# Hybrid GLA, attention and RG-LRU backbone on one core: the recurrent blocks' input scale by another formula, and separate waits for their two gate buffers

## The reference, cut to what matters

```python
def lru_coeffs(x, w_gates, b_gates, lam):
    xb = x.reshape(b, n, LRU_BLOCKS, LRU_BW)                 # 8 blocks of 128 channels
    z = jnp.einsum('bnhi,ghij->gbnhj', xb, w_gates).reshape(2, b, n, w) + b_gates[:, None, None, :]
    gate_r, gate_i = jax.nn.sigmoid(z[0]), jax.nn.sigmoid(z[1])
    log_a = -LRU_C * gate_r * jax.nn.softplus(-lam)
    u = jnp.sqrt(-jnp.expm1(2.0 * log_a)) * (gate_i * x)
    return jnp.exp(log_a), u
# and then, per channel and in each of the two directions: h = a * h + u
```

## Time and profile before

| what | value |
|---|---|
| time, median of 3 runs (lowest to highest) | 2126.31 us (2124.08 to 2127.26) |
| the profiled execution: its own time / its span | 2122.79 us / 2121.0 us |
| mean granted TensorE clock | 0.973 |
| PE busy | 1978.5 us, 93% of the span |
| DVE busy | 1132.7 us, 53% |
| ACT busy | 939.3 us, 44% |
| POOL busy | 48.9 us, 2% |

### The profile page before, as it was taken

One profiled execution on the slowest core, in us unless ns is written; L12 is line 12 of the kernel. 1 busy time (PEld: TensorE's weight loads), 2 busy tenths in 40 slices (PEclk: granted clock), 3 DMA queues, 4 the chain that ended last, 5 costly groups with the idle time before them and its releaser, 6 DMA issues.

```text
span 2121.0 us, 26328 instructions
## 1 busy us (share of the span) xinstructions
PE 1978.5 (93%) x10944; PEld 1608.7 (76%) x10944; DVE 1132.7 (53%) x1615; ACT 939.3 (44%) x1301; POOL 48.9 (2%) x65
## 2 busy tenths in 40 slices
PE   4999999999999999699999998899899988989997
PEld 1878766777787777477777785778677887979997
DVE  2566455544645432555555324675555667657864
ACT  2343344454644322333333323443344777446653
POOL 1000000000000000000000000000000101000000
PEclk8999999999999999899999999999999999999999
DMA  7211111132333544245444522222212444544563
GB/s 283 60 60 50 55 50 40 50 98 91 99 95 102 175 172 160 78 143 175 169 159 162 177 90 79 60 70 60 66 60 74 150 144 135 170 129 155 184 185 104
DMA packets 67511, 244.98 MB, mean 116 GB/s; under 512 B 7600, under 2 KB 8640, under 8 KB 67264
## 3 DMA queue, kind: packets, MB, share of 16 engines
q1 hardware_dynamic: 64544, 233.86, 33.8%
q0 software_dynamic: 1696, 5.24, 0.8%
q10 hardware_dynamic: 1152, 4.19, 0.5%
HBM read 242.21 MB, written 1.05 MB: 115 GB/s over the span
## 4 chain that ended last, share of the span: by engine, by line
PE 81%; DVE 10%; ACT 5%; issue 2%; DMA 1%; SPq 0%; ACTq 0%; DVEq 0%
PE ps L1258 62%; PE ps L1248 4%; PE ps L1534 2%; PE ps L1189 2%; PE ps L1444 2%; DVE wlo L742 1%; PE ps L1278 1%; DMA wraw<-in_weights 1%; ACT whi L399 1%; DVE state L1002 1%; PE ps L1465 1%; PE ps L1198 1%; PE ps L1358 1%; PE ps L1368 1%; PE ps L1345 1%
## 5 line engine op out<-in xcount | busy, mean ns | idle before, releaser
L742 DVE TENSOR_TENSOR wlo<-wraw,whi 128x1024 fp32r<-128x1024 f32 x352 | 433.4, 1233 | 517.0 <-ACT whi L399 516.5
L399 ACT ACTIVATE whi<-wraw 128x1024 fp32r<-128x1024 f32 x352 | 370.5, 1055 | 387.4 <-PE ps L1258 241.1
L1258 PE MATMUL ps<-hh,whi 128*128 128x512 f32 (+1 forms) x1760 | 415.9, 359 | 33.2 <-DVE hl L859 23.9
L1258 PE MATMUL ps<-hl,whi 128*128 128x512 f32 (+1 forms) x1760 | 398.9, 349 | 0.0
L1258 PEld LDWEIGHTS ps<-hh,whi 128*128 128x128 f32 x1760 | 292.7, 193 | 109.5 <-issue 65.5
L1258 PE MATMUL ps<-hh,wlo 128*128 128x512 f32 (+1 forms) x1760 | 366.5, 349 | 1.6 <-DVE wlo L742 1.6
L1258 PEld LDWEIGHTS ps<-hl,whi 128*128 128x128 f32 x1760 | 296.2, 193 | 42.1 <-issue 1.9
L1258 PEld LDWEIGHTS ps<-hh,wlo 128*128 128x128 f32 x1760 | 287.2, 192 | 44.1 <-issue 4.4
L770 DVE SCALAR_TENSOR_TENSOR fa<-ps,par,fa 128x510 f32<-128x510 f32 (+1 forms) x176 | 100.0, 610 | 14.9 <-ACT fa L462 13.4
L1258 PE MATMUL ps<-bh,whi 128*128 128x512 f32 (+1 forms) x384 | 85.8, 346 | 4.4 <-ACT whi L399 4.4
L462 ACT ACTIVATE fa<-ps,par 128x512 f32<-128x512 f32 (+1 forms) x88 | 53.9, 663 | 69.6 <-PE ps L1258 69.5
(11 more groups left out here) (206 smaller groups left out, 2424.7 us busy)
## 6 DMA issues: line engine op xcount, KB each, us to landing
wraw<-in_weights SPq DMA_DIRECT2D x352, 512.0 KB, 3.6
wada<-in_w_ada SPq DMA_DIRECT2D x80, 512.0 KB, 4.1
ada_first<-in_w_ada ACTq DMA_DIRECT2D x8, 512.0 KB, 18.7
ada_first<-in_w_ada SPq DMA_DIRECT2D x8, 512.0 KB, 20.1
wgate<-in_w_gate POOLq DMA_DIRECT2D x16, 256.0 KB, 2.8
x<-in_xt SPq DMA_DIRECT2D x1, 2048.0 KB, 10.1
out_x<-x SPq DMA_DIRECT2D x1, 1024.0 KB, 4.5
par<-in_params POOLq DMA_DIRECT2D x1, 370.0 KB, 9.4
```

The costliest lines, as they stand in the source:

```text
L399: A_(whi[u % HI][:], wraw[RING_W[u] % RAW][:], ACT.Copy).then_inc(s_hi, 1)
L742: V.tensor_tensor(wlo[s][:], wraw[s][:], whi[u % HI][:].bitcast(F32), ALU.subtract).then_inc(s_lo, 1)
L1258: ins = mm(dst[:, r, c:], w[:, kk, r * P:(r + 1) * P], x_[:, UK * h + kk, c:], start=h == 0 and k in (0, 2) and kk == 0, stop=h == m - 1 a ...
```

## The change

Three parts. First, the formula: `l_th` becomes tanh(-x/2) (its scale is `k2`, from a new column product in the layer's prologue), ACT takes the root of -`l_th`/4 at once, and DVE multiplies that by (1 + a). The square on POOL is gone, with its semaphore. Second, the order: `lru_sqrt` waits only for ACT's own tanhs; `l_ti` = (`l_ti` + 1) x moves into `lru_in`, one pair earlier on DVE; `lru_v` now holds the product with (1 + a) and waits for the root. Third, the waits: the `l_tr` tanhs wait for the product in `lru_h` (`s_lin`), and only the `l_ti` tanhs for `s_lh`; the four tanhs are ordered by buffer and no longer by direction.

```diff
                     if n < BLOCKS - 1:
                         pool.wait_ge(s_lz, 2 * b + 2)
                         pool.dma_start(wgate[:], w_gate[b + 1]).then_inc(s_gate, 16)
-                    pool.wait_ge(s_lt, b + 1)
-                    nc.gpsimd.tensor_tensor(l_tr[:], l_a[:], l_a[:], ALU.mult).then_inc(s_la2, 1)
...
                 def lru_tanhs(n):
                     b = BLOCKS * l + n
-                    act.wait_ge(s_lh, b) if b else None
-                    for d in range(2):
-                        act.wait_ge(s_lz, 2 * b + d + 1)
-                        for g, buf in enumerate((l_tr, l_ti)):
+                    act.wait_ge(s_lin, b) if b else None
+                    for g, buf in enumerate((l_tr, l_ti)):
+                        if g and b:
+                            act.wait_ge(s_lh, b)
+                        for d in range(2):
+                            act.wait_ge(s_lz, 2 * b + d + 1) if g == 0 else None
                             t = 4 * n + 2 * d + g
                             ins = A_(buf[:, d], ps[:, 4 + 2 * d + g], ACT.Tanh, scale=0.5, bias=hbias[:, t:t + 1])
-                        ins.then_inc(s_ltz, 1)
+                            if g:
+                                ins.then_inc(s_ltz, 1)
 
                 def lru_exps(n):
                     b = BLOCKS * l + n
                     act.wait_ge(s_ltz, 2 * b + 2)
                     for d in range(2):
-                        k4 = sp[:, 2, 2 * n + d:2 * n + d + 1]
+                        k4, k2 = (sp[:, j, 2 * n + d:2 * n + d + 1] for j in (2, 1))
                         A_(l_a[:, d], l_tr[:, d], ACT.Exp, scale=k4, bias=k4)
-                        ins = A_(l_th[:, d], l_tr[:, d], ACT.Tanh, scale=k4, bias=k4)
+                        ins = A_(l_th[:, d], l_tr[:, d], ACT.Tanh, scale=k2, bias=k2)
                     ins.then_inc(s_lt, 1)
 
                 def lru_sqrt(n):
-                    act.wait_ge(s_lv, BLOCKS * l + n + 1)
-                    A_(l_tr[:], l_tr[:], ACT.Sqrt, scale=-0.25).then_inc(s_ls, 1)
+                    act.wait_ge(s_lt, BLOCKS * l + n + 1)
+                    A_(l_tr[:], l_th[:], ACT.Sqrt, scale=-0.25).then_inc(s_ls, 1)
...
                 link(V.tensor_tensor(sp[:, 0], sp[:, 0], sp[:, 1], ALU.add))
+                V.tensor_scalar(sp[:, 1], sp[:, 0], -2.0, None, ALU.mult)
                 V.tensor_scalar(sp[:, 2], sp[:, 0], -4.0, None, ALU.mult).then_inc(s_c4, 1)
...
-                def lru_v(n):
-                    b = BLOCKS * l + n
-                    dve.wait_ge(s_la2, b + 1)
-                    V.scalar_tensor_tensor(l_tr[:], l_tr[:], 1.0, l_th[:], ALU.add, ALU.mult).then_inc(s_lv, 1)
+                def lru_in(n):
+                    dve.wait_ge(s_ltz, 2 * (BLOCKS * l + n) + 2)
                     link(V.scalar_tensor_tensor(l_ti[:], l_ti[:], 1.0, xc[:, n, None].broadcast_to([P, 2, TOK]),
                                                 ALU.add, ALU.mult))
+
+                def lru_v(n):
+                    dve.wait_ge(s_ls, BLOCKS * l + n + 1)
+                    link(V.scalar_tensor_tensor(l_tr[:], l_a[:], 1.0, l_tr[:], ALU.add, ALU.mult))
 
                 def lru_h(n):
                     b = BLOCKS * l + n
                     l_h = l_th
-                    dve.wait_ge(s_ls, b + 1)
-                    link(V.tensor_tensor(l_ti[:], l_ti[:], l_tr[:], ALU.mult))
+                    V.tensor_tensor(l_ti[:], l_ti[:], l_tr[:], ALU.mult).then_inc(s_lin, 1)
+                    dve.wait_ge(s_lin, b + 1)
                     V.tensor_tensor_scan(l_h[:, 0], l_a[:, 0], l_ti[:, 0], 0.0, ALU.mult, ALU.add)
...
                     if a - 2 in LRU_AT:
                         lru_v(LRU_AT.index(a - 2))
                     edge(u3 + 2 * a + 1)
+                    if a - 1 in LRU_AT:
+                        lru_in(LRU_AT.index(a - 1))
                     if a - 2 in LRU_AT:
                         lru_h(LRU_AT.index(a - 2))
```

More of the change, by code:

```diff
@@ L252, in build @@
         s_ahi, s_alo = sem("att_hi"), sem("att_lo")
-        s_lz, s_ltz, s_lt, s_la2 = sem("lru_logits_done"), sem("lru_logits_taken"), sem("lru_exps_made"), sem("lru_squares")
-        s_lv, s_ls, s_lh = sem("lru_v_made"), sem("lru_sqrt_made"), sem("lru_h_made")
+        s_lz, s_ltz, s_lt = sem("lru_logits_done"), sem("lru_logits_taken"), sem("lru_exps_made")
+        s_lin, s_ls, s_lh = sem("lru_inputs_made"), sem("lru_sqrt_made"), sem("lru_h_made")
         s_c_act, s_c_dve = sem("act_chain"), sem("dve_chain")
```

## The result

| what | before | after |
|---|---|---|
| time, median of the runs (lowest to highest) | 2126.64 us (2124.08 to 2127.26, 4 runs) | 2110.32 us (2108.57 to 2111.82, 4 runs) |
| the profiled execution: its own time / its span | 2122.79 / 2121.0 us | 2108.57 / 2106.7 us |
| mean granted TensorE clock | 0.973 | 0.976 |
| busy: PE, DVE, ACT, POOL | 1978.5, 1132.7, 939.3, 48.9 us | 1975.7, 1130.2, 940.5, 18.3 us |

The account below looks back on a forecast made before the run. PE, busy 93%, bounds the kernel; its layer 1 waits can go: -3.5 - 5.0 - 2.7 - 3.7 - 2.4 (slow clock) + 0.2 = -17.1, less 0.8 for remaining slow clock, -16.3: 2110.0 us. Range 2103.5 to 2119.

Parts of the forecast that it names:

- Where the time is: Layer 1's recurrent stage: 22.7 us of PE waiting and slow clock can be won; in layer 0 PE does not wait.
- Groups 1 and 2: First two runs of five pairs with two blocks, layer 1's recurrent stage: all 3.5 and 5.0 us lost come back.
- Group 3: Third five pairs of layer 1's stage, ACT's fullest stretch: 2.7 of 6.6 us come back, 3.9 of PE waits stay.
- Group 4: Last five pairs of layer 1's stage: 3.7 us come back, 1.5 of idle stays before the unit waiting for `ev`.
- Prologue: Start of each layer: one more product of 16 columns costs 0.2 us in layer 1, nothing counted in layer 0.
- w: ACT's wait for DVE between the root's table load and the root, 1.21 to 1.97 us; claimed to go as a whole.
- first rival: Root's table load has a tail hidden by the old wait: 1.2 us of each w stays, time 2117.2; chance 0.12.
- Nothing moves: The `hi` ring of three ties ACT and DVE to PE, so gains are waited for again: 2124 to 2128; chance 0.09.
- all idle goes: ACT's and DVE's queues in layer 1's stage are less tight than counted; all 22.7 us return: 2103.8; chance 0.12.
- third rival: Waits change engine: `lru_v` holds DVE behind the root, PE waits for `wlo`: 2138, or about 2132; chance 0.05.
- the margin: `lo` behind the root's product is ready 1.4 us after `hi`, PE asks at 1.9: 0.5 us to spare.
- The square: POOL's square of `l_a` beside DVE's `lo`: at most 6 us of DVE time back, no term of its own.

Follow-up runs that it names:

- e1: Kernel before plus only the split wait of the tanhs (old formula, POOL's square and root's wait for DVE stay): 2120.49 us, ratio 0.9978.
- e2: Kernel after with all four tanhs waiting for the sum again, so new formula and order alone: 2115.70 us, ratio 0.9947.
- e3: Kernel after with the product for `l_ti` (`lru_in`) directly behind the root's product on DVE: 2117.60 us, ratio 0.9958.
- e5: Kernel after with `lru_in` directly ahead of `lru_v`, so ahead of DVE's wait for the root: 2109.85 us, ratio 0.9922.
- e7: Kernel after with POOL's unused square put back and one wait, for POOL, ahead of the root: 2109.79 us, ratio 0.9918.
- e4: Kernel after with POOL's unused square put back and two waits ahead of the root: 2113.40 us, ratio 0.9937.
- after_again: The kernel after, unchanged, measured again beside the kernel before: 2110.04 us, ratio 0.9924.

## Why the prediction was right

*Where the time is.* PE idle and slow clock in layer 1's recurrent stage, and nothing in layer 0. Right: the stage gave 14.5 us, and 2.4 of slow clock behind it went too. The gates of layer 0's blocks start at 429.36 us before and 429.21 after, the last ones at 638.45 and 638.29: 209.1 us both times. One reading was off by a little: the 4.62 us of the chain for the unit at 1672.50 are 4.44 from start to start in the timeline, so its slow clock is 1.6 us and not 1.7.

*Groups 1 and 2.* 3.5 and 5.0 us forecast, 3.5 and 5.0 measured, and the `hi` of group 2 is just in time, as counted. e1 and e2 show that group 1 needs only the root, and group 2 both edits.

*Group 3.* 3.9 us left were forecast, 4.2 measured, but not made up as I had said. The 0.4 for `hi` and the 2.1 for `wlo` are there (0.35 and 1.83). The 0.9 and 0.5 for the two `hi` around block 5's root are not. The slow clock behind the 1.83 stretched PE's next unit to 3.97 us (1742.13 to 1746.10), and in that time ACT caught up. I had set 0.8 us for such a stretch on top of the waits; it came with some 1.6, in place of 1.4 of waiting. Two errors cancel here, and the agreement of the sum is better than its terms deserve.

*Group 4.* 37.2 forecast, 37.2 measured; idle of 1.5 forecast, 1.43 measured.

*Prologue.* +0.2 forecast, 0.08 measured. The sum was wrong: two such products overlap, and the second starts 0.09 us behind the first, not 0.20. From the start of the sum of `sp` to the first fill of `lrh` DVE takes 0.54 us before (1324.70 to 1325.24) and 0.62, 0.61 and 0.61 in the three traces of the kernel after. It is too small for the times.

*The chain by blocks.* The root had w = 0 behind its load, so the first rival (a hidden tail of the load) is refuted by eight roots with 0.1 us of idle together. The drain that the Trainium skill counts with a switch of tables ("ScalarE: Activation LUTs", What ACT_TABLE_LOAD costs) does not show here as idle before the next activation: the root starts 0.01 us behind its load, as the gate tanh did. "Nothing moves" falls with the gates' distances, and "all idle goes" with what is left in groups 3 and 4. The third rival's mechanism exists, as e3 shows, with the margin that I had given; the change stays on the right side of it by placing `lru_in` ahead of the wait for the root. A whole pair earlier would not have been needed, as e5 shows.

*The square.* I gave its removal no term. e7 bears that out: 0.3 us of stage.

*From the stage to the time.* The two profiled executions differ by 14.2 us, the medians by 16.3. Of the 17 us around the stage, 2.8 were given back in the profiled run before it began: its first gates start at 1640.48 instead of 1637.71. That is not the change. From the last gates of layer 0 to the sum of `sp` in the prologue of layer 1 it is 686.3 us before and 687.7 after, and from there to the first gates of layer 1 313.0 and 314.5; but in the other two traces of the kernel after the same stretches take 686.4 and 686.1, and 313.2 and 312.9, as before. The forecast of the difference, 16.3, was met to the decimal, and that is luck: the other two pairs of medians lie 16.1 and 18.3 us apart, the ratio gives 15.5, and the profiled execution, forecast at 2106.5, took 2108.6.

## What to carry to other kernels

When an engine that prepares operands for the bottleneck waits inside its queue for a third engine, count the time from that wait to the next operand that the bottleneck needs: two waits of one to three microseconds in a block, on an engine that was busy for less than half of the span, cost 0.7% here. Reformulate so that an engine's next instruction reads what that engine made itself, and split a wait on a shared set of buffers by the last reader of each buffer. After such an edit, look at what now stands behind the new wait: the same product costs 0.4 us directly ahead of it, against a place a pair earlier, and 7 us behind it.

## What the hardware showed that I had not expected

*A wait's place beside a table load.* With one semaphore to wait for, the table load ran ahead of the wait; with two, ACT waited for POOL ahead of the load (0.62 us of idle before the load of 1.28). So in this kernel a second wait ahead of an activation cost the cover that the load gives: 5.2 us of ACT and 2.5 us of stage, between e4 and e7.

*Where the noise of this kernel comes from.* Twelve traces of kernels that have nearly the same work ahead of layer 1's recurrent stage reach it between 1637.71 and 1644.36 us. Most of that is there early: the first gates of layer 0 start between 428.49 and 433.26 us. In the first 75 us the traces differ in what the transfers move and in PE's clock; in the first 25 us, 368 GB/s in the kernel after and 349 in after_again, in the next 25 a clock of 0.83 and 0.66. Which of these is the cause stays open.

A second part is the moment at which PE's clock falls and rises around waits that are the same. One window, 1500 to 1550 us, with the same waits of PE, in the kernel before and the kernel after:

```profile
1500.00:1550.00 50.00, 39.16 (x219) 0.97 0.23 69
```

```profile
1500.00:1550.00 50.00, 39.16 (x209) 0.93 0.20 59
```

The length from the sum of `sp` to the first gates of layer 1, a stretch that holds this window, goes with that clock in all twelve traces: 312.9 to 313.2 us in the five with 0.97, 314.3 to 314.5 in the six with 0.93, and 314.7 in the one with 0.90, e2_root_only. So the lower clock costs 1.4 us there, in all of these kernels alike. Edits worth one or two microseconds must be read from the length of their stage, not from the time of the kernel.
